# Rows of the moving operand padded to 2304 bytes per two chunks, and the high-weight products of a tile taken in the order xh, xh, xl, xl

## The chip, the cores and the metric

The kernel runs on one core of one Trainium2 chip. The metric is the device time of one execution in microseconds (us); lower is better. The times given are medians over several executions, and beside them stands one profiled execution with its own time.

## The reference

The kernel computes one inference step of a decoder with two layers for 256 prompt tokens and 8 sample tokens, which are handled together as 264 columns. Almost all of the work is products of float32 weights with activations of width 2048 (5632 in the hidden layer):

```python
h = rms_norm(x, norm_mix[layer])
z = h @ w_in                       # even layer 2048x4608, odd layer 2048x4112
y = mixer(z) @ w_out               # 2048x2048; attention+conv, or linear attention+pooling
x = x + y
h = rms_norm(x, norm_ffn[layer])
x = x + (silu(h @ w_gate) * (h @ w_up)) @ w_down     # 2048x5632, 2048x5632, 5632x2048
```

Each weight is used once for all 264 columns. It streams from HBM in float32.

## The kernel before

Activations stand with the features on the 128 partitions: a chunk is 128 features, and its row on each partition has T = 264 numbers of 4 bytes, 1056 bytes. An activation of width 2048 has 16 chunks, the hidden one has 44. To keep the accuracy of float32 each operand is split into a high part (rounded to the matmul's format `F32R`) and the rest: `xh` and `xl` for the normalised input, `hh` and `hl` for the input of the output projections and of the down projection, `whi` and `wlo` for the weights. Three products are summed: high weight by high activation, high weight by low activation, low weight by high activation.

The weights come in units. A unit is two chunks of the contraction by 512 output features (512 KB), loaded by SyncE's queue into one of four slots of `raw`; ScalarE writes its high part (`split_hi`, L404), VectorE the rest (`split_lo`, L413). TensorE then runs `unit`: for each of the four tiles `t` of 128 output features it issues four high-weight products (L514), over the two chunks `kk` and within each over the high and the low activation, and after the four tiles eight low-weight products (L520) follow, two per tile. So a unit has 16 + 8 = 24 matmuls of 128x128 weights by a 128x264 moving operand, each with its own weight load. Units that end a group with `single` set run the low products of a tile right behind its high ones. The sum of a tile stays in one PSUM bank over all units of its group: 8 units where the input has 16 chunks, 22 in the down projection. Index `j` below is the place of a unit in its group; it reads chunks 2j and 2j+1.

All buffers are placed by hand with `put`, one after another from byte 1024 of a partition:

```python
x = put("x", [P, KC, T], 1024)
xh_t = put("xh", [P, KC, T], after("x"), F32R)
xl_t = put("xl", [P, KC, T], after("xh"), F32R)
raw = put("raw", [P, RING, 2 * COLS], after("xl"))
```

This gives, with 1056 = 4 x 256 + 32 bytes a chunk, the byte offsets xh 17920 (70 x 256), xl 34816 (136 x 256), raw 51712, whi 68096 (266 x 256), wlo 84480, hh 100864 (394 x 256), hl 147328 (575 x 256 + 128). So chunk c of xh and of xl starts 32c bytes behind a multiple of 256, that of hh too, and that of hl 128 + 32c bytes behind one. Every weight tile starts at a multiple of 256.

The order of the work on each engine is the order of the code. TensorE waits at a unit for `hi_done` before the high products and for `lo_done` before the low ones.

Of the kernel before, what the change touches and what calls it, by code (L numbers as in the profile page):

```python
# [27 lines left out]
F32R = mybir.dt.float32r  # L28
# [6 lines left out]
P = 128  # L35
D = 2048
TP, NB = 256, 8
T = TP + NB
KC = D // P
# [9 lines left out]
PB = 15  # L49
COLS = 512  # L50
RING = 4
AHEAD = 3


# [80 lines left out]
def decoder_step(nc, a, o):  # L135
# [6 lines left out]
    with ctx:  # L142
        def sem(name):
            return ctx.enter_context(nc.semaphore(name))
# [5 lines left out]
        def put(name, shape, at, dt=F32):  # L150
            size = 1
            for s in shape[1:]:
                size *= s
            size *= 2 if dt == BF16 else 4
            used[name] = (at, at + size)
            return nc.alloc_sbuf_tensor_at(name, shape, dt, offset=at)

        def after(name):
            return (used[name][1] + 31) // 32 * 32

        x = put("x", [P, KC, T], 1024)
        xh_t = put("xh", [P, KC, T], after("x"), F32R)
        xl_t = put("xl", [P, KC, T], after("xh"), F32R)
        xh, xl = ([z[:, c, :] for c in range(KC)] for z in (xh_t, xl_t))
        raw = put("raw", [P, RING, 2 * COLS], after("xl"))
        whi = put("whi", [P, RING, 2 * COLS], after("raw"), F32R)
        wlo = put("wlo", [P, RING, 2 * COLS], after("whi"), F32R)
        hh = put("hh", [P, FC, T], after("wlo"), F32R)
# [79 lines left out]

        raw_full = [sem(f"raw_full{s}") for s in range(RING)]
        raw_up = [sem(f"raw_up{s}") for s in range(RING)]  # L250
        hi_done = sem("hi_done")
# [117 lines left out]
        def at_turn(eng, i, step, first):  # L369

            if i is None:
                return first
            return i * step + first if isinstance(i, int) else eng.snap(i * step + first)


        def pieces(buf, n, split=False):

            slot = buf[:, n % RING, :]  # L380
            if n >= U_EVEN + 2 * IN_UNITS:
# [8 lines left out]
        def split_hi(act, n, i=None, step=0, up=None):  # L390

            if beyond(n, i, step):
                return
            landed = at_turn(act, i, 16 * step // RING, 16 * (n // RING + 1))
            if up is not None:
                up = at_turn(act, i, up[1], up[0])
            free = at_turn(act, i, step, n - RING + 1)
            act.wait_ge(raw_full[n % RING], landed)
            if up is not None:
                act.wait_ge(raw_up[n % RING], up)  # L400
            if n >= RING:
                act.wait_ge(units_done, free)
            for dst, src in zip(pieces(whi, n, True), pieces(raw, n)):
                ins = act.activation(dst, src, ACT.Copy)  # L404
            ins.then_inc(hi_done, 1)
# [96 lines left out]
        def _(pe):  # L502
            def unit(n, yhi, ylo, k0, bank, first, last, i=None, step=0, taken=None, single=False):


                s = n % RING
                by_tile = single and last
                pe.wait_ge(lo_done if by_tile else hi_done, at_turn(pe, i, step, n + 1))

                def hi_part(t):  # L510
                    for kk in range(2):
                        c = kk * COLS + t * P
                        for m, r in enumerate((yhi, ylo)):
                            pe.matmul(ps[:, bank + t, 0:T], whi[:, s, c:c + P], r[k0 + kk],  # L514
                                      start=first and kk == 0 and m == 0, stop=False)

                def lo_part(t):
                    for kk in range(2):
                        c = kk * COLS + t * P
                        mm = pe.matmul(ps[:, bank + t, 0:T], wlo[:, s, c:c + P], yhi[k0 + kk],  # L520
                                       start=False, stop=last and kk == 1)
                    return mm

                for t in range(4):
                    if taken is not None and t < 3:
                        pe.wait_ge(evac_t, taken[0] + t)
                    if taken is not None and t == 3:
                        pe.wait_ge(evac_g, taken[1])
                    hi_part(t)
                    if by_tile:  # L530
                        mm = lo_part(t)
                        if t < 3:
                            mm.then_inc(tile_done, 1)
                if not by_tile:
                    pe.wait_ge(lo_done, at_turn(pe, i, step, n + 1))
                    for t in range(4):
                        mm = lo_part(t)
                mm.then_inc(units_done, 1)
# [393 lines left out]
        def _(act):  # L932
# [14 lines left out]
            def norm_prep(m, g, taken, base):  # L947

                c0 = 4 * g
                if m:  # L950
                    act.wait_ge(evac_g, taken)
                else:
                    act.wait_ge(d_x[g], 16)
                for t in range(2 if m == g == 0 else 0, 4):
                    ins = act.activation(xh[c0 + t], x[:, c0 + t, :], ACT.Copy, scale=vec[:, base + c0 + t:base + c0 + t + 1])  # L955
                ins.then_inc(xh_done, 1)
                if m or g > 1:
                    act.wait_ge(acc_done, 3 * m + max(g - 1, 0))
                act.activation(sqs[:, min(g, 1), :, :].rearrange("p c t -> p (c t)"),
                               x[:, c0:c0 + 4, :].rearrange("p c t -> p (c t)"), ACT.Square).then_inc(sq_done, 1)  # L960
# [59 lines left out]
            for u in range(EVEN_GROUPS * IN_UNITS):  # L1020
                n = U_EVEN + u + AHEAD
                split_hi(act, n)
# [73 lines left out]
            def out_proj(U, G, m, base, split_rows):  # L1096
                for q in range(4):
                    for j in range(IN_UNITS):
                        up = (16 * (q + 1), 0) if split_rows and (j + AHEAD) in ATTN_UNITS else None
                        split_hi(act, U + IN_UNITS * q + j + AHEAD, up=up)  # L1100
                    norm_prep(m, q, G + q + 1, base)

            def ffn(layer, U, G, m):
                def gate_up(i, peeled):
                    for k in range(2 * IN_UNITS):
                        split_hi(act, U + k + AHEAD, i=i, step=2 * IN_UNITS)
                        if peeled and k == 5:
# [12 lines left out]
                if layer == 0:  # L1120
                    for q in range(4):
                        for j in range(DN_UNITS):
                            split_hi(act, U2 + DN_UNITS * q + j + AHEAD)
                        norm_prep(2, q, G2 + q + 1, V_MIX + KC)
                    return

                for k in range(4 * DN_UNITS):
                    split_hi(act, U2 + k + AHEAD)
                    q, at = divmod(k, DN_UNITS)
# [729 lines left out]
```

## Time and profile before

| what | value |
|---|---|
| time, median of 3 | 2267.44 us (2267.36 to 2268.8) |
| time of the profiled execution | 2266.24 us |
| its span, first to last instruction | 2264.5 us |
| TensorE busy | 99% of the span |
| VectorE, ScalarE busy | 54%, 42% |
| granted TensorE clock, mean | 0.995 |
| matmuls | 18226 |

The span is the time in which the profile sees instructions; the time of the same execution is 1.74 us longer. A matmul is listed with its own duration (some 0.28 us), but matmuls overlap: what one costs in a stream is the distance from its start to the start of the next.

### The profile page before, as it was taken

What the parts mean: (1) busy time and instruction counts of PE and PEld (TensorE: products, weight loads), DVE (VectorE), ACT (ScalarE), POOL (GpSimd) and SP (SyncE); (2) the same over time, 40 slices, a digit from 0 to 9 for tenths busy, and PEclk for the clock granted to TensorE, in tenths of its full rate; (3) what the DMA queues carried; (4) which work ended last, traced back from release to release, by engine and by line L of the source; (5) the groups of instructions that cost most, each with busy time, mean ns of one, the idle gap of its engine ahead of it and who ended that gap; (6) DMA issues with size and microseconds to landing.
All of it is one profiled execution on the core that took longest, in us unless ns stands there. A gap on an engine that the chain in (4) does not pass through costs nothing.

```text
span 2264.5 us, 43613 instructions
## 1 busy us (share of the span) xinstructions
PE 2245.3 (99%) x18226; PEld 2222.4 (98%) x18226; DVE 1218.8 (54%) x1294; ACT 952.6 (42%) x1059; POOL 18.0 (1%) x20
## 2 busy tenths in 40 slices
PE   7999999999999999999999999999999999999999
PEld 7999999999999999999999999999999999999999
DVE  5777656555555554444465466565555555544443
ACT  6545345334343433433353335453434334343332
POOL 0000000000000000000000020000000000000000
PEclk9999999999999999999999999999999999999999
DMA  6654465655556565555564485556565655655654
GB/s 209 234 172 135 138 187 170 192 178 180 181 178 184 167 193 178 180 175 185 186 196 143 127 247 162 181 178 185 168 192 169 189 181 177 185 178 191 190 186 132
DMA packets 217579, 405.13 MB, mean 179 GB/s; under 512 B 15440, under 2 KB 29392, under 8 KB 217312
## 3 DMA queue, kind: packets, MB, share of 16 engines
q1 hardware_dynamic: 201360, 384.94, 55.0%
q10 hardware_dynamic: 16112, 18.63, 2.5%
q8 instruction: 83, 1.36, 0.2%
q14 instruction: 24, 0.20, 0.0%
HBM read 395.67 MB, written 9.93 MB: 179 GB/s over the span
## 4 chain that ended last, share of the span: by engine, by line
PE 97%; DVE 1%; ACT 1%; issue 0%; DMA 0%; SPq 0%; ACTq 0%; DVEq 0%
PE ps L514 62%; PE ps L520 31%; PE ps L848 1%; PE ps L819 0%; PE ps L816 0%; DMA raw<-in_w_in_even 0%; PE ps L858 0%; DVE wlo L413 0%; ACT whi L404 0%; PE ps L595 0%; PE ps L886 0%; PE ps L613 0%; PE ps L604 0%; PE ps L549 0%; ACT xh L955 0%
## 5 line engine op out<-in xcount | busy, mean ns | idle before, releaser
L413 DVE TENSOR_TENSOR wlo<-raw,whi 128x1024 fp32r<-128x1024 f32 (+1 forms) x746 | 886.0, 1202 | 837.2 <-ACT whi L404 836.2
L404 ACT ACTIVATE whi<-raw 128x1024 fp32r<-128x1024 f32 (+1 forms) x746 | 765.3, 1038 | 913.6 <-PE ps L520 902.2
L514 PE MATMUL ps<-xh,whi 128*128 128x264 f32 x3904 | 984.9, 288 | 10.1 <-ACT whi L404 9.1
L514 PE MATMUL ps<-xl,whi 128*128 128x264 f32 x3904 | 976.7, 285 | 0.0
L514 PEld LDWEIGHTS ps<-xh,whi 128*128 128x128 f32 x3904 | 740.6, 190 | 17.7 <-DVE xl L1335 8.5
L514 PEld LDWEIGHTS ps<-xl,whi 128*128 128x128 f32 x3904 | 741.6, 190 | 0.7
L520 PE MATMUL ps<-xh,wlo 128*128 128x264 f32 x3904 | 564.7, 285 | 0.0
L520 PEld LDWEIGHTS ps<-xh,wlo 128*128 128x128 f32 x3904 | 513.1, 189 | 0.0
L514 PE MATMUL ps<-hh,whi 128*128 128x264 f32 x1920 | 477.3, 284 | 1.1 <-DVE gbuf L1325 1.1
L514 PE MATMUL ps<-hl,whi 128*128 128x264 f32 x1920 | 477.2, 284 | 0.0
L514 PEld LDWEIGHTS ps<-hh,whi 128*128 128x128 f32 x1920 | 361.1, 188 | 1.3 <-issue 1.3
L514 PEld LDWEIGHTS ps<-hl,whi 128*128 128x128 f32 x1920 | 361.1, 188 | 0.0
L520 PE MATMUL ps<-hh,wlo 128*128 128x264 f32 x1920 | 273.0, 284 | 0.0
L520 PEld LDWEIGHTS ps<-hh,wlo 128*128 128x128 f32 x1920 | 250.1, 188 | 0.0
L1114 ACT ACTIVATE hh<-ubuf 128x1056 f32 (+1 forms) x22 | 23.9, 1087 | 101.3 <-DVE ubuf L1559 101.3
L1111 ACT ACTIVATE gbuf<-gbuf 128x1056 f32<-128x1056 f32 x22 | 23.9, 1087 | 66.5 <-DVE gbuf L1552 66.5
L1562 DVE TENSOR_TENSOR hl<-ubuf,hh 128x1056 f32 (+1 forms) x22 | 27.7, 1258 | 30.1 <-ACT hh L1114 30.1
L955 ACT ACTIVATE xh<-x,vec 128x264 fp32r<-128x264 f32 x62 | 26.9, 504 | 37.2 <-DVE x L1522 37.2
L1292 DVE SCALAR_TENSOR_TENSOR xl<-x,vec,xh 128x264 fp32r<-128x264 f32 x62 | 26.5, 489 | 22.6 <-ACT xh L955 22.6
L1554 DVE TENSOR_TENSOR ubuf<-ps,rstd 128x1056 f32<-128x1056 f32 x22 | 27.7, 1258 | 12.9 <-PE ps L520 12.9
L1552 DVE TENSOR_TENSOR gbuf<-ps,rstd 128x1056 f32<-128x1056 f32 x22 | 27.7, 1257 | 11.9 <-PE ps L520 11.9
L1559 DVE TENSOR_TENSOR ubuf<-ubuf,gbuf 128x1056 f32<-128x1056 f32 x22 | 27.7, 1258 | 2.5
(210 smaller groups left out, 582.2 us busy)
## 6 DMA issues: line engine op xcount, KB each, us to landing
raw<-in_w_gate SPq DMA_DIRECT2D x176, 512.0 KB, 4.0
raw<-in_w_up SPq DMA_DIRECT2D x176, 512.0 KB, 4.3
raw<-in_w_down SPq DMA_DIRECT2D x176, 512.0 KB, 3.7
raw<-in_w_in_even SPq DMA_DIRECT2D x72, 512.0 KB, 4.1
raw<-in_w_in_odd SPq DMA_DIRECT2D x66, 512.0 KB, 3.7
raw<-in_w_out_odd SPq DMA_DIRECT2D x32, 512.0 KB, 4.0
raw<-in_w_out_even SPq DMA_DIRECT2D x16, 512.0 KB, 4.5
raw<-in_w_out_even SPq DMA_DIRECT2D x32, 256.0 KB, 4.2
```

The lines of the kernel that those rows point to most:

```text
L404: ins = act.activation(dst, src, ACT.Copy)
L413: ins = dve.tensor_tensor(dst, src, hi.bitcast(F32), ALU.subtract)
L514: pe.matmul(ps[:, bank + t, 0:T], whi[:, s, c:c + P], r[k0 + kk], start=first and kk == 0 and m == 0, stop=False)
L520: mm = pe.matmul(ps[:, bank + t, 0:T], wlo[:, s, c:c + P], yhi[k0 + kk], start=False, stop=last and kk == 1)
L955: ins = act.activation(xh[c0 + t], x[:, c0 + t, :], ACT.Copy, scale=vec[:, base + c0 + t:base + c0 + t + 1])
L1111: act.activation(gbuf[:, :, :], gbuf[:, :, :], ACT.Silu).then_inc(silu_done, 1)
L1114: act.activation(dst, ubuf[:, :, :], ACT.Copy).then_inc(hh_done, 1)
L1292: ins = dve.scalar_tensor_tensor(xl[c], x[:, c, :], vec[:, base + c:base + c + 1], xh[c].bitcast(F32), ALU.mult, ALU.subtract)
L1552: dve.tensor_tensor(gbuf[:, :, :], ps[:, 0:4, 0:T], scale, ALU.mult).then_inc(evac_g, 1)
L1554: dve.tensor_tensor(ubuf[:, :, :], ps[:, 4:8, 0:T], scale, ALU.mult).then_inc(evac_g, 1)
L1559: dve.tensor_tensor(ubuf[:, :, :], ubuf[:, :, :], gbuf[:, :, :], ALU.mult).then_inc(h_ready, 1)
L1562: dve.tensor_tensor(hl[:, at, :], ubuf[:, :, :], hh[:, at, :].bitcast(F32), ALU.subtract).then_inc(hid_done, 1)
```

## The change

The rows of `xh` and `xl` are put in pairs of chunks, and each pair takes 576 numbers (2304 = 9 x 256 bytes) in place of 528 (2112 bytes). Each of the two buffers grows by 1536 bytes, and every buffer behind xh moves: xl starts at 36352 (142 x 256) and all behind it 3072 (12 x 256) bytes further. In `unit`, the two loops of the high products change places.

```diff
+PAIR = 576
...
-        xh_t = put("xh", [P, KC, T], after("x"), F32R)
-        xl_t = put("xl", [P, KC, T], after("xh"), F32R)
-        xh, xl = ([z[:, c, :] for c in range(KC)] for z in (xh_t, xl_t))
+        xh_t = put("xh", [P, KC // 2, PAIR], after("x"), F32R)
+        xl_t = put("xl", [P, KC // 2, PAIR], after("xh"), F32R)
+        xh, xl = ([z[:, c // 2, (c % 2) * T:(c % 2 + 1) * T] for c in range(KC)] for z in (xh_t, xl_t))
...
                 def hi_part(t):
-                    for kk in range(2):
-                        c = kk * COLS + t * P
-                        for m, r in enumerate((yhi, ylo)):
+                    for m, r in enumerate((yhi, ylo)):
+                        for kk in range(2):
+                            c = kk * COLS + t * P
                             pe.matmul(ps[:, bank + t, 0:T], whi[:, s, c:c + P], r[k0 + kk],
                                       start=first and kk == 0 and m == 0, stop=False)
```

After the change an even chunk of xh or xl starts at a multiple of 256 bytes and an odd one 32 bytes behind one, whatever the pair. The starts of hh and hl within 256 bytes stay what they were.

On TensorE, the end of the first unit of the even layer's input projection (the last tiles' high products, the low products, the start of the next unit) was this before; xh and xl are the two parts of the input, whi and wlo those of the weights:

```order
L514 MATMUL ps<-xl,whi 128x264
L514 MATMUL ps<-xh,whi 128x264
L514 MATMUL ps<-xl,whi 128x264
L514 MATMUL ps<-xh,whi 128x264
L514 MATMUL ps<-xl,whi 128x264
L520 MATMUL ps<-xh,wlo 128x264 x8
L514 MATMUL ps<-xh,whi 128x264
```

It is this after the change:

```order
L515 MATMUL ps<-xh,whi 128x264 x2
L515 MATMUL ps<-xl,whi 128x264 x2
L515 MATMUL ps<-xh,whi 128x264 x2
L515 MATMUL ps<-xl,whi 128x264 x2
L521 MATMUL ps<-xh,wlo 128x264 x8
L515 MATMUL ps<-xh,whi 128x264 x2
```

The two chunks of xh now come one after the other, then the two of xl; the same weight tile is no longer used by two matmuls in a row, and the eight low products keep their place.

The same place in the output projection of the even layer, on TensorE, where hh and hl are the two parts of the activation, was this before:

```order
L514 MATMUL ps<-hl,whi 128x264
L528 REGISTER_ALU
L514 MATMUL ps<-hh,whi 128x264
L514 MATMUL ps<-hl,whi 128x264
L514 MATMUL ps<-hh,whi 128x264
L514 MATMUL ps<-hl,whi 128x264
L520 MATMUL ps<-hh,wlo 128x264 x8
```

It is this after the change:

```order
L515 MATMUL ps<-hl,whi 128x264 x2
L529 REGISTER_ALU
L515 MATMUL ps<-hh,whi 128x264 x2
L515 MATMUL ps<-hl,whi 128x264 x2
L521 MATMUL ps<-hh,wlo 128x264 x8
```

Here only the order moved; the rows of hh and hl are not padded.

## Rows read from the trace of the kernel before

**Rows 1.** The page: busy time by engine, and TensorE's granted clock in 40 slices.

```profile
span 2264.5 us, 43613 instructions
PE 2245.3 (99%) x18226; PEld 2222.4 (98%) x18226; DVE 1218.8 (54%) x1294; ACT 952.6 (42%) x1059; POOL 18.0 (1%) x20
PEclk9999999999999999999999999999999999999999
```

**Rows 2.** The page's costliest groups: busy us, mean ns | idle before, releaser.

```profile
L413 DVE TENSOR_TENSOR wlo<-raw,whi 128x1024 fp32r<-128x1024 f32 (+1 forms) x746 | 886.0, 1202 | 837.2 <-ACT whi L404 836.2
L404 ACT ACTIVATE whi<-raw 128x1024 fp32r<-128x1024 f32 (+1 forms) x746 | 765.3, 1038 | 913.6 <-PE ps L520 902.2
...
L520 PE MATMUL ps<-xh,wlo 128*128 128x264 f32 x3904 | 564.7, 285 | 0.0
...
L520 PE MATMUL ps<-hh,wlo 128*128 128x264 f32 x1920 | 273.0, 284 | 0.0
```

**Rows 3.** Waits of TensorE: engine line, waited for, us in total, times, longest.

```profile
PE ps L514 <- ACT whi L404: 9.1, 2, 8.5
```

**Rows 4.** Timeline of TensorE, gate projection, units j = 0 to 5: start us, us.

```profile
435.78 0.28 PE L514 MATMUL ps<-xh,whi 128*128 128x264 f32 x1
...
437.70 1.13 PE L520 MATMUL ps<-xh,wlo 128*128 128x264 f32 x8
438.67 0.28 PE L514 MATMUL ps<-xh,whi 128*128 128x264 f32 x1
...
440.61 1.14 PE L520 MATMUL ps<-xh,wlo 128*128 128x264 f32 x8
441.58 0.29 PE L514 MATMUL ps<-xh,whi 128*128 128x264 f32 x1
...
443.54 1.15 PE L520 MATMUL ps<-xh,wlo 128*128 128x264 f32 x8
444.52 0.28 PE L514 MATMUL ps<-xh,whi 128*128 128x264 f32 x1
...
447.43 0.28 PE L514 MATMUL ps<-xh,whi 128*128 128x264 f32 x1
...
449.36 1.13 PE L520 MATMUL ps<-xh,wlo 128*128 128x264 f32 x8
450.32 0.28 PE L514 MATMUL ps<-xh,whi 128*128 128x264 f32 x1
```

**Rows 5.** Timeline of TensorE, down projection: units j = 20, 21, then 0 to 3.

```profile
937.04 0.28 PE L514 MATMUL ps<-hh,whi 128*128 128x264 f32 x1
...
939.94 0.28 PE L514 MATMUL ps<-hh,whi 128*128 128x264 f32 x1
...
942.85 0.28 PE L514 MATMUL ps<-hh,whi 128*128 128x264 f32 x1
...
944.79 1.12 PE L520 MATMUL ps<-hh,wlo 128*128 128x264 f32 x8
945.76 0.28 PE L514 MATMUL ps<-hh,whi 128*128 128x264 f32 x1
...
947.68 1.14 PE L520 MATMUL ps<-hh,wlo 128*128 128x264 f32 x8
948.66 0.29 PE L514 MATMUL ps<-hh,whi 128*128 128x264 f32 x1
...
950.61 1.14 PE L520 MATMUL ps<-hh,wlo 128*128 128x264 f32 x8
951.59 0.28 PE L514 MATMUL ps<-hh,whi 128*128 128x264 f32 x1
...
953.56 1.14 PE L520 MATMUL ps<-hh,wlo 128*128 128x264 f32 x8
954.54 0.28 PE L514 MATMUL ps<-hh,whi 128*128 128x264 f32 x1
```

## The prediction, made before the result was known

> **What bounds the kernel now.** I read the page first. TensorE is busy 99% of the span and its granted clock is at the upper level in all 40 slices; VectorE and ScalarE are busy 54% and 42% [rows 1]. The groups say whose turn it is: the high split of the weights on ScalarE was idle 902.2 us waiting for TensorE's low products, and VectorE 836.2 us waiting for that split [rows 2]. Both splitters run at TensorE's pace. TensorE itself waited for a split twice, 9.1 us in all, 8.5 of them in one wait [rows 3]. So the end is set by how fast matmuls follow one another, and nothing else that this change touches can give or take much unless TensorE begins to wait.
>
> How fast do they follow? The timeline shows it, by the distances of starts. In the gate projection six units start at 435.78, 438.67, 441.58, 444.52, 447.43 and 450.32 [rows 4]: 2.89, 2.91, 2.94, 2.91 and again 2.89 us for 24 matmuls each, although each does the same work on the same shapes. In the down projection units j = 0 to 3 take 2.91, 2.90, 2.93 and 2.95 us [rows 5]. The one thing that runs in a cycle of four units is the place of the rows within 256 bytes: chunk c starts 32c bytes behind a multiple of 256, so units of j = 0 and 4 read rows at 0 and 32, j = 1 at 64 and 96, j = 2 at 128 and 160, j = 3 at 192 and 224.
>
> Is it the rows' place, or a beat of four that TensorE keeps by itself? The down projection tells: its group has 22 units, no multiple of four. Units 20 and 21 take 2.90 and 2.91 us, and then the next group's j = 0 and 1 take 2.91 and 2.90 us; a beat of its own would have gone on with the 2.93 and 2.95 us that come two units later [rows 5]. The pattern starts anew with the rows. I read it so: what one matmul costs depends, by some per cent of 121 ns, on where its moving row and its neighbours' begin within 256 bytes.
>
> **The change part by part.**
>
> *Padding.* After it every unit on xh and xl reads rows at 0 and 32, as only the units j = 0 and 4 do today. A cycle of four units takes 447.43 - 435.78 = 11.65 us, 2.9125 a unit; the two units with rows at 0 and 32 take 2.89 and 2.89 [rows 4]. The number of units on xh is 3904 low products by 8 = 488 [rows 2]. At 2.89 us for all the gain is 0.0225 x 488 = 11.0 us. The starts are given to 0.01 us, so this term is good to about 0.005 x 488 = 2.4 us.
>
> *Order, on xh and xl.* The high products now read rows at 0, 32, 0, 32 with a new weight tile each time. That is exactly the pattern of the eight low products today. With rows at 0 and 32 those take 438.67 - 437.70 = 0.97 and 450.32 - 449.36 = 0.96 us [rows 4], 0.965 on average; three times that is a unit of 2.895 us. Today's order gives 2.89. I take 2.893: a gain of 0.0195 x 488 = 9.5 us. Giving up the repeated weight tile costs nothing visible: high products that repeat theirs and low ones that do not run alike, (437.70 - 435.78) / 16 = 0.120 us against 0.965 / 8 = 0.121.
>
> *Order, on hh and hl.* These rows do not move within 256 bytes, but the order is new: with hl 128 bytes off, a tile reads rows at 0, 128, 32, 160 today and at 0, 32, 128, 160 afterwards (j = 0; the others shifted). No row of this trace shows that order. The nearest rows: today's high products take 1.94, 1.92, 1.95 and 1.97 us for j = 0 to 3, mean 1.945; the low ones, another order of the same rows, take 0.97, 0.98, 0.98, 0.98, mean 0.978, which is 1.955 for sixteen [rows 5]; and the high ones on xh, a third order, take 1.92, 1.94, 1.96 in the units j = 0 to 2 [rows 4]. Three orders average to within 1% of each other, so I take no change. The bounds are the best and the worst single unit, 1.92 and 1.97 us, for all of the 1920 / 8 = 240 units [rows 2]: 6 us less or 6 us more.
>
> *The shift of all buffers behind xh* is 3072 bytes, a multiple of 256; by the reading above it costs nothing. The pairs j = 0 and j = 4 lie 8448 bytes apart, a multiple of 256 but of no higher power of two, and take the same 2.89 us [rows 4]; so the address bits above 256 have shown no effect. If they had, it would come as in the no-change rival.
>
> *What else.* No wait is added and no instruction either: the writers of xh and xl write rows of the same length, the transfers are the same, and which sum closes when is unchanged. With a unit 0.02 us shorter, the splitters have less idle time: a whi split takes 1.038 us and a wlo split 1.202 us a unit [rows 2], far below 2.89; their idle time covers it 80 times over.
>
> The sum: 9.5 us off the profiled execution's 2266.24 gives 2256.7; the median of the runs lies 1.2 us above that execution, so I expect 2257.9 us, 0.4% faster.
>
> **A rule that speaks against it.** The trace shows matmuls of 264 columns 2.89 / 24 = 0.120 to 2.94 / 24 = 0.1225 us apart by the rows they read [rows 4]. The Trainium skill, "TensorE: Matmul & The Clock Gate", section "Back-to-back issue gap", makes the distance a matter of the column count alone. Its formula, as an estimate from that page, gives 112.5 ns for 264 columns; the trace does not agree, with 120 ns at the least. By that rule the padding would do nothing and the time would stay at 2267.4 us; the first rival is that outcome.
>
> **The rivals.**
>
> *No change.* The cause of the cycle is not the row's place within 256 bytes but something that goes with it, such as the distance between row and weight tile or the two buffers' distance, which the new layout does not reproduce; then units average 2.9125 us as now and the time is 2267.4 us. For it: I have only a pattern, no mechanism. Against it: units 20 and 21 against 0 and 1, and j = 0 against j = 4. The Trainium skill, "SBUF — State Buffer", section "Specifications (TRN2)", speaks of lines of 16 bytes only; by them rows that all start at multiples of 32 are alike. The trace does not agree, by 2.89 against 2.94 us.
>
> *Slower.* The mechanism is the order: where two matmuls in a row no longer share a weight tile, and the row alternates between places, each high product falls to the slowest pace seen, 1.97 us for sixteen [rows 5]. A unit on xh would take 1.97 + 0.965 = 2.935 us, 0.0225 more than now, times 488 = 11.0 us; a unit on hh 1.97 in place of 1.945, times 240 = 6 us; together 2284 us. It decides from 2.9125 - 0.965 = 1.9475 us for the sixteen high products of an xh unit, against the 1.93 I expect. For it: on hh the order is unseen. Against it: the low products have this very form and are not slow at 0 and 32.
>
> *Larger gain.* The new order also avoids the slow neighbours on hh, and each of its units takes the 1.92 us of the best: 6 us more, and with 2.89 on xh 1.5 more, gives 2250.4 us. For it: hl stands 128 bytes off hh, and today's order jumps between them at each matmul. Against it: the low products never jump and are no faster.
>
> **How the numbers follow.** A measurement of this kernel tells about 0.2%, 4.5 us, from no change. The forecast, 2257.9, has a chance of 0.60; its own range is 2253 to 2263, from 2.4 us of rounding and half of the 6 us of the order on hh. The larger gain has 0.18, no change 0.13, slower 0.09. The range 2249 to 2266 takes in the forecast, the larger gain, and losses on hh that eat most of the gain; it leaves out 2267 and above. Faster 0.77: nearly all of the first two cases, less a little where hh takes its 6 us; same 0.14; slower 0.09.
>
> **What would show it.** After the change the starts of units on xh should be 2.89 to 2.90 us apart for every j, without the cycle of four. If the cycle is still there, the place within 256 bytes is not the cause. If the cycle is gone but at 2.91 or more, the order costs. On hh the low products should still take 0.97 to 0.98 us, and the high ones an average of 1.945; a new average there is the order's own effect. The clock should stay at the upper level and TensorE's wait for the splits near 9 us; more of it would mean that I was wrong about what covers them. The prediction fails most simply if hh loses what xh gains.

## The result, and the profile after

The changed kernel takes 2256.45 us (median of 5, 2254.95 to 2259.57) against 2267.39 us (median of 5); the ratio is 0.9955, interval 0.9944 to 0.9966. It is 0.45% or 10.9 us faster; 2257.9 us was forecast, 0.4%. The range held the time and the sign was right. One reason behind it was not, as the experiments show.

The profiled execution took 2259.57 us, one of the longer ones. Its page, where the lines of [rows 1] stand, reads:

```profile
span 2257.8 us, 43613 instructions
PE 2237.8 (99%) x18226; PEld 2214.4 (98%) x18226; DVE 1217.8 (54%) x1294; ACT 952.4 (42%) x1059; POOL 18.1 (1%) x20
PEclk9999999999999999999999899999999999999999
```

TensorE is still the bound, with the same 18226 matmuls. A 9 in the clock's row stands for 90% or more of a slice, so neither this row nor that of [rows 1] shows whether the clock fell for a few microseconds. TensorE's waits for the high split are as small as in [rows 3], 9.4 us in two waits.

From here on one reading serves for all kernels: the start of a unit of the gate projection, and the start of the one 64 units later; and the start of the down projection's first unit, and that of the one 44 units (two whole groups) later. Their distances divided by 64 and by 44 are the mean unit on xh and on hh, good to a fraction of a nanosecond. The timeline of TensorE in the kernel before (start us, us) has, beside the start at 435.78 of [rows 4]:

```profile
622.23 0.28 PE L514 MATMUL ps<-xh,whi 128*128 128x264 f32 x1
...
878.61 0.28 PE L514 MATMUL ps<-hh,whi 128*128 128x264 f32 x1
...
1007.09 0.28 PE L514 MATMUL ps<-hh,whi 128*128 128x264 f32 x1
```

That is 186.45 / 64 = 2.9133 us a unit on xh and 128.48 / 44 = 2.9200 on hh. The same view of the changed kernel:

```profile
434.76 0.28 PE L515 MATMUL ps<-xh,whi 128*128 128x264 f32 x1
...
619.08 0.28 PE L515 MATMUL ps<-xh,whi 128*128 128x264 f32 x1
...
872.52 0.28 PE L515 MATMUL ps<-hh,whi 128*128 128x264 f32 x1
...
1001.60 0.29 PE L515 MATMUL ps<-hh,whi 128*128 128x264 f32 x1
```

A unit on xh takes 184.32 / 64 = 2.8800 us, 120.0 ns a matmul; one on hh 129.08 / 44 = 2.9336, more than before. With all units of a kind taken like the ones measured, the 488 units on xh give 0.0333 x 488 = 16.3 us and the 240 on hh take back 0.0136 x 240 = 3.3 us: 13.0 us net.

The two profiled executions differ by 6.7 us only. The windows say where the rest is. Their columns are: stretch, length, TensorE busy (matmuls), granted clock, DMA share, GB/s. Before the change:

```profile
240.00:280.00 40.00, 40.00 (x312) 0.91 0.44 121
1225.00:1300.00 75.00, 75.00 (x525) 0.93 0.39 120
```

After it:

```profile
240.00:280.00 40.00, 40.00 (x298) 0.87 0.45 123
1225.00:1300.00 75.00, 75.00 (x502) 0.86 0.39 119
```

These are the two places where the stream of projections is mixed with the mixers' small products, and the clock falls there to its lower level (1.2 GHz) for some microseconds, in both kernels; from 245.10 to 248.30 us the kernel before had a granted clock of 0.50. If TensorE does half as much in that time, a stretch loses its length times the missing share: 40 x 0.09 + 75 x 0.07 = 8.9 us before and 40 x 0.13 + 75 x 0.14 = 15.7 after, 6.8 us more in this execution. Taken from the 13.0 us this leaves 6.2, and 6.7 was measured. The mean clocks of the five runs of the changed kernel were 0.992 to 0.994, its shortest run having the highest; a few microseconds of this kind differ from run to run.

### The profile page after: what moved, and what is told of

Same layout as the page of the kernel before. It is cut to its first block, busy times and chain, and to the rows that moved or that the text cites. A ratio compares the mean times of both kernels' runs of the same rounds, so it can differ in the third digit from the quotient of the medians.

```text
span 2257.8 us, 43613 instructions
## 1 busy us (share of the span) xinstructions
PE 2237.8 (99%) x18226; PEld 2214.4 (98%) x18226; DVE 1217.8 (54%) x1294; ACT 952.4 (42%) x1059; POOL 18.1 (1%) x20
## 4 chain that ended last, share of the span: by engine, by line
PE 96%; DVE 1%; ACT 1%; DMA 1%; issue 0%; SPq 0%; ACTq 0%; DVEq 0%
PE ps L515 61%; PE ps L521 30%; DMA raw<-in_w_in_even 1%; PE ps L849 1%; PE ps L820 0%; PE ps L817 0%; ACT whi L405 0%; DVE wlo L414 0%; PE ps L859 0%; PE ps L596 0%; PE ps L887 0%; PE ps L614 0%; PE ps L605 0%; PE ps L550 0%; ACT xh L956 0%
## 5 line engine op out<-in xcount | busy, mean ns | idle before, releaser
L515 PE MATMUL ps<-xh,whi 128*128 128x264 f32 x3904 | 802.2, 287 | 10.7 <-ACT whi L405 9.4
L515 PE MATMUL ps<-xl,whi 128*128 128x264 f32 x3904 | 794.1, 285 | 0.0
L515 PEld LDWEIGHTS ps<-xh,whi 128*128 128x128 f32 x3904 | 606.7, 190 | 19.1 <-DVE xl L1336 8.3
L515 PEld LDWEIGHTS ps<-xl,whi 128*128 128x128 f32 x3904 | 605.5, 190 | 0.0
L521 PE MATMUL ps<-xh,wlo 128*128 128x264 f32 x3904 | 559.0, 284 | 0.0
L521 PEld LDWEIGHTS ps<-xh,wlo 128*128 128x128 f32 x3904 | 507.3, 189 | 0.0
L515 PE MATMUL ps<-hh,whi 128*128 128x264 f32 x1920 | 391.3, 285 | 1.3 <-DVE gbuf L1326 1.3
L515 PE MATMUL ps<-hl,whi 128*128 128x264 f32 x1920 | 391.4, 285 | 0.0
L515 PEld LDWEIGHTS ps<-hh,whi 128*128 128x128 f32 x1920 | 298.3, 189 | 1.5 <-issue 1.5
L515 PEld LDWEIGHTS ps<-hl,whi 128*128 128x128 f32 x1920 | 298.6, 189 | 0.0
```

## The experiments

A time with an interval is a median of several; where one time stands alone, the unit times, which do not depend on the clock's falls elsewhere, are the better measure. A "place" is the start of a row in bytes behind a multiple of 256.

### Padding alone, order alone

`pad_only` is the changed kernel with the old loops:

```diff
-                    for m, r in enumerate((yhi, ylo)):
-                        for kk in range(2):
-                            c = kk * COLS + t * P
+                    for kk in range(2):
+                        c = kk * COLS + t * P
+                        for m, r in enumerate((yhi, ylo)):
```

> The padded rows with the old order xh, xl, xh, xl. Theory 1 (the rows' place within 256 bytes alone sets the pace): every unit on xh at 2.88 to 2.89 us, units on hh unchanged at 2.91, 2.90, 2.93, 2.95; time 2255 to 2257 us, at or below the changed kernel since hh loses nothing. Theory 2 (place and order act together): units on xh at 2.89 us as today's j = 0, of which the order takes another 0.012 us in the changed kernel; time about 2257.

Measured: 2266.1 us, ratio 0.9998, interval 0.9989 to 1.0007. The padding alone gives nothing. Timeline of TensorE:

```profile
434.99 0.28 PE L515 MATMUL ps<-xh,whi 128*128 128x264 f32 x1
...
436.94 1.12 PE L521 MATMUL ps<-xh,wlo 128*128 128x264 f32 x8
437.90 0.28 PE L515 MATMUL ps<-xh,whi 128*128 128x264 f32 x1
...
621.44 0.28 PE L515 MATMUL ps<-xh,whi 128*128 128x264 f32 x1
```

186.45 / 64 = 2.9133 us a unit, to the digit the mean of before. But the cycle of four is gone: the unit shown takes 437.90 - 434.99 = 2.91, and so do the others. The low products are at their best (0.96 us for eight), the sixteen high ones take 1.95 where the same rows in the same order took 1.92 before the change [rows 4, j = 0]. So both theories were wrong here. The rows' places count, since the cycle went with them, but the two rows of a unit do not settle what it takes. Either what was read before it counts too (unit j = 0 of the unpadded kernel comes behind the places 192 and 224), or the distance between the buffers does; `old_apart_512` and `hl_place_timed` below decide.

`order_only` is the kernel before with the new loops.

> The new order with unpadded rows. Theory 1 (place alone): the cycle of four stays on xh with a mean of 2.91 us, and hh goes to the 2.93 us of the changed kernel; time 2269 to 2271 us. Theory 2 (the order by itself quickens units, place hardly counts): units on xh near 2.88 us without a cycle, time about 2257 us.

Measured: 2270.0 us, ratio 1.0015, interval 1.0006 to 1.0024: slower by 0.15%, in the range of theory 1.

```profile
436.65 0.28 PE L514 MATMUL ps<-xh,whi 128*128 128x264 f32 x1
...
623.31 0.28 PE L514 MATMUL ps<-xh,whi 128*128 128x264 f32 x1
...
879.98 0.28 PE L514 MATMUL ps<-hh,whi 128*128 128x264 f32 x1
...
888.79 0.41 PE L514 MATMUL ps<-hh,whi 128*128 128x264 f32 x2
...
891.72 0.41 PE L514 MATMUL ps<-hh,whi 128*128 128x264 f32 x2
...
1009.12 0.29 PE L514 MATMUL ps<-hh,whi 128*128 128x264 f32 x1
...
1017.89 0.40 PE L514 MATMUL ps<-hh,whi 128*128 128x264 f32 x2
...
1020.79 0.41 PE L514 MATMUL ps<-hh,whi 128*128 128x264 f32 x2
```

Units on xh take 186.66 / 64 = 2.9166 us, those on hh 129.14 / 44 = 2.935. Neither edit gives anything alone; together they give 16 us on xh. The loss on hh belongs to the order.

Two things here go beyond theory 1. On xh the cycle has eight units, not four: j = 2 starts at 442.48 and j = 3 at 445.42 (2.94 us), but j = 6 at 454.12 and j = 7 at 457.08 (2.96 us), with rows at the same places; it comes back in every group. And on hh the same unit has two times. The first and the third group of the down projection read the same rows from the same slots into the same banks, yet the first four units take 891.72 - 879.98 = 11.74 us in the one and 1020.79 - 1009.12 = 11.67 us in the other, and the fourth of them still 2.93 against 2.90. Apart from the values of the weights, only what ran before differs: the up projection, or another group on hh. So its effect reaches over at least three whole units, 72 matmuls.

### New order on xh, old order on hh

`order_x_only` is the changed kernel with the choice made by the operand:

```diff
-                    for m, r in enumerate((yhi, ylo)):
-                        for kk in range(2):
+                    for kk, m in (((0, 0), (1, 0), (0, 1), (1, 1)) if yhi is xh else ((0, 0), (0, 1), (1, 0), (1, 1))):
+                            r = (yhi, ylo)[m]
```

> Padded rows; new order for units on xh, old order for units on hh. If the two kinds of units are independent: xh units 2.880 us as in the changed kernel, hh units 2.92 us on average as before, so 0.01 us x 240 = 2.5 us below the changed kernel: about 2254 us. If the loss on hh came from the moved buffers and not from the order, hh units stay at 2.93 us and the time is that of the changed kernel, 2256.

Measured: 2252.09 us, ratio 0.9930, interval 0.9917 to 0.9944.

```profile
434.54 0.28 PE L515 MATMUL ps<-xh,whi 128*128 128x264 f32 x1
...
618.86 0.28 PE L515 MATMUL ps<-xh,whi 128*128 128x264 f32 x1
...
872.30 0.28 PE L515 MATMUL ps<-hh,whi 128*128 128x264 f32 x1
...
1000.79 0.28 PE L515 MATMUL ps<-hh,whi 128*128 128x264 f32 x1
```

184.32 / 64 = 2.8800 us on xh and 128.49 / 44 = 2.9202 on hh: the gain on xh without the loss on hh. The moved buffers have no part in the loss on hh.

### Place against what?

`place_128` moves the rows of xh and xl by 128 bytes and leaves the weights where they are within 256 bytes; `all_128` moves everything behind x by 128:

```diff
-        xh_t = put("xh", [P, KC // 2, PAIR], after("x"), F32R)
+        xh_t = put("xh", [P, KC // 2, PAIR], after("x") + 128, F32R)
...
-        raw = put("raw", [P, RING, 2 * COLS], after("xl"))
+        raw = put("raw", [P, RING, 2 * COLS], after("xl") + 128)     # place_128 only
```

> The changed kernel with xh and xl begun 128 bytes further, so that all pairs have rows at 128 and 160; weights and hh stay at their places within 256. If the place relative to the weights or to the 256 bytes counts: units on xh rise from 2.880 towards the 2.94 us of today's j = 2, all alike, and the time to about 2275 us or less. If only the equality of all pairs counts, they stay at 2.880 us and the time at 2256.

> The changed kernel with every buffer behind x 128 bytes further, weights and hh too. If the place counts relative to the weight tiles: units on xh at 2.880 us and the four units on hh unchanged (2.946, 2.927, 2.937, 2.937 us for j = 0 to 3), time 2257 us. If the place counts by itself: xh units at 2.960 us as in the kernel with the rows alone moved, the values of hh rotated by two, time about 2284 us.

Measured, one time each: 2283.76 us with the rows alone moved, 2253.92 us with everything moved. TensorE's timeline with the rows alone moved:

```profile
438.21 0.29 PE L515 MATMUL ps<-xh,whi 128*128 128x264 f32 x1
...
627.65 0.29 PE L515 MATMUL ps<-xh,whi 128*128 128x264 f32 x1
```

With everything moved:

```profile
431.98 0.28 PE L515 MATMUL ps<-xh,whi 128*128 128x264 f32 x1
...
616.30 0.28 PE L515 MATMUL ps<-xh,whi 128*128 128x264 f32 x1
...
869.74 0.28 PE L515 MATMUL ps<-hh,whi 128*128 128x264 f32 x1
...
998.81 0.29 PE L515 MATMUL ps<-hh,whi 128*128 128x264 f32 x1
```

189.44 / 64 = 2.960 us against 184.32 / 64 = 2.8800, and hh at 129.07 / 44 = 2.9334, the value of the changed kernel. So it is not the row's own address that counts but its place against the weight tiles, which moved along in the second kernel and not in the first. The slow case is slower than expected: 2.960 us is more than the 2.94 of any unit in [rows 4], and 2283.76 us more than the 2275. Equal pairs alone are no merit, since at places 128 and 160 all units are equally slow.

### The distance of the buffers

`apart_512` is the changed kernel with `put("xl", ..., after("xh") + 512)`, `old_apart_512` is `pad_only` with the same. They were to say why sixteen high products took 1.92 us at j = 0 before and 1.95 with the padding alone.

> The changed kernel with xl and all behind it 512 bytes further, so that xl starts 18944 bytes behind xh (512 more than a multiple of 2048, as before the change) and not 18432 (a multiple of 2048). Theory 3 (the distance of two rows read in turn counts by its bits above 256): units on xh rise from 2.880 to the 2.906 us that the order-only kernel had at j = 0, in every unit, 0.026 x 488 = 12.7 us in all, about 2269 us. Theory 1 (place within 256 bytes alone, given the order): 2.880 us and about 2257 us.

> Padded rows, old order, xl 512 bytes further. Theory 3: each unit on xh takes the 2.892 us of j = 0 before the change, in place of 2.913 with the padding alone; 0.021 x 488 = 10 us, about 2256 us. If the distance has no part in it: 2.913 us and 2266 us.

Measured, one time each: 2255.86 and 2269.34 us. Timeline of `apart_512`:

```profile
432.47 0.28 PE L515 MATMUL ps<-xh,whi 128*128 128x264 f32 x1
...
616.79 0.28 PE L515 MATMUL ps<-xh,whi 128*128 128x264 f32 x1
```

And of `old_apart_512`:

```profile
436.16 0.28 PE L515 MATMUL ps<-xh,whi 128*128 128x264 f32 x1
...
622.62 0.28 PE L515 MATMUL ps<-xh,whi 128*128 128x264 f32 x1
```

184.32 / 64 = 2.8800 and 186.46 / 64 = 2.9134 us, both unchanged. Theory 3 fell: 512 bytes more between the buffers do nothing. Other distances were not tried.

### hl at the same place as hh

`hl_place` is `order_x_only` with one more edit:

```diff
-        hl = put("hl", [P, FC, T], after("hh"), F32R)
+        hl = put("hl", [P, FC, T], after("hh") + 128, F32R)
```

> New order on xh and old order on hh, with hl begun 128 bytes further, so that a chunk of hl stands at the same place within 256 bytes as that of hh. If hh then behaves as xh did before the change (same places, old order): 2.913 us a unit on average in place of 2.920, 0.007 x 240 = 1.7 us less than the kernel it is built from, about 2250.5 us. If the new distance between hh and hl is a worse one: 2.93 us or more, about 2255 us.

> The kernel with new order on xh, old order on hh and hl moved by 128 bytes, timed in rounds. By its units (2.880 us on xh, 2.9135 on average on hh and hl) against those before (2.9135 and 2.9215): 0.0335 x 488 + 0.008 x 240 = 18.3 us less, 2249 us.

Measured: 2248.01 us (one time), and for the same kernel as `hl_place_timed` 2248.39 us, ratio 0.9915, interval 0.9902 to 0.9929. The timeline of the latter:

```profile
432.03 0.28 PE L515 MATMUL ps<-xh,whi 128*128 128x264 f32 x1
...
616.35 0.28 PE L515 MATMUL ps<-xh,whi 128*128 128x264 f32 x1
...
869.79 0.28 PE L515 MATMUL ps<-hh,whi 128*128 128x264 f32 x1
...
881.46 0.28 PE L515 MATMUL ps<-hh,whi 128*128 128x264 f32 x1
...
884.35 0.28 PE L515 MATMUL ps<-hh,whi 128*128 128x264 f32 x1
...
933.88 0.29 PE L515 MATMUL ps<-hh,whi 128*128 128x264 f32 x1
...
936.79 0.28 PE L515 MATMUL ps<-hh,whi 128*128 128x264 f32 x1
...
997.97 0.29 PE L515 MATMUL ps<-hh,whi 128*128 128x264 f32 x1
```

128.18 / 44 = 2.913 us on hh. With the same places and the same order hh takes what xh took before the change, 2.9133. 128 unused bytes are worth 0.007 x 240 = 1.7 us.

The same lines show what `pad_only` left in doubt. Unit j = 4 starts at 881.46, behind one with rows at 192 and 224, and takes 2.89 us. Unit j = 0 of the second group starts at 933.88, behind j = 21 with rows at 64 and 96, and takes 2.91. Both read rows at 0 and 32 in the same order, in one kernel: a unit's time depends on what was read before it.

`hl_place_new_order` has the new order everywhere on top of this layout.

> The new order on all units, padded xh and xl, hl moved by 128 bytes. Theory 4 (the sequence of places within 256 bytes, relative to the weight tile, sets the pace, whatever the buffer): units on hh take what the order-only kernel took on unpadded xh, 2.906, 2.928, 2.960, 2.886 us for j = 0 to 3, mean 2.920; time 2250 us. If the buffer or its distance mattered: other values, such as the 2.937 us of the changed kernel, and 2254 us.

Measured: 2249.05 us (one time).

```profile
869.77 0.28 PE L515 MATMUL ps<-hh,whi 128*128 128x264 f32 x1
...
998.12 0.28 PE L515 MATMUL ps<-hh,whi 128*128 128x264 f32 x1
```

128.35 / 44 = 2.917 us, which is the 2.9166 of unpadded xh in the new order. Theory 4 holds: the same sequence of places gives the same time, whichever buffer it is. The values expected for single j did not come one by one, since the cycle has eight units here too, as in `order_only`.

### Cheaper padding

`x_blocks` is `hl_place` with xh and xl in blocks of four chunks, 1088 numbers each, begun 192 bytes further, so that units alternate between places 192, 224 and 0, 32. It asks whether a third of the padding would do.

```diff
-        xh_t = put("xh", [P, KC // 2, PAIR], after("x"), F32R)
+        xh_t = put("xh", [P, KC // 4, 4 * T + 32], after("x") + 192, F32R)
...
+        xh, xl = ([z[:, c // 4, (c % 4) * T:(c % 4 + 1) * T] for c in range(KC)] for z in (xh_t, xl_t))
+        raw = put("raw", [P, RING, 2 * COLS], after("xl") + 64)
```

> xh and xl in blocks of four chunks, 4352 = 17 x 256 bytes each, begun 192 bytes behind a multiple of 256: even units read rows at 192 and 224, odd units at 0 and 32, for 1024 bytes of padding a buffer pair of 2048 less than the changed kernel's. Theory 4a (each of these two pairs of places runs at 120 ns and a switch between them costs nothing lasting): 2.880 to 2.886 us a unit, about 2248 us. Theory 4b (a switch costs, as in the order-only kernel, where j = 0 took 2.906 us after j = 3): up to 2.906 us a unit, 0.02 x 488 = 10 us more, about 2258 us.

Measured: 2258.14 us (one time).

```profile
432.21 0.28 PE L515 MATMUL ps<-xh,whi 128*128 128x264 f32 x1
...
435.11 0.41 PE L515 MATMUL ps<-xh,whi 128*128 128x264 f32 x2
...
438.02 0.41 PE L515 MATMUL ps<-xh,whi 128*128 128x264 f32 x2
...
618.02 0.28 PE L515 MATMUL ps<-xh,whi 128*128 128x264 f32 x1
```

185.81 / 64 = 2.9033 us: theory 4b. Changing the pair of places from unit to unit costs 0.023 us a unit, two thirds of the gain. It is not that only the pair 192 and 224 is slow: the unit from 435.11 to 438.02 reads rows at 0 and 32 and takes 2.91 us, where it takes 2.88 when all units read there. No run has 192 and 224 alone.

### Sequence of places or repeated weight tile?

The new order differs from the old in two things: the places alternate, and no weight tile is used twice in a row. `side_by_side` parts them. It is `hl_place` with the old order everywhere and this layout:

```diff
-        xh_t = put("xh", [P, KC // 2, PAIR], after("x"), F32R)
-        xl_t = put("xl", [P, KC // 2, PAIR], after("xh"), F32R)
-        xh, xl = ([z[:, c // 2, (c % 2) * T:(c % 2 + 1) * T] for c in range(KC)] for z in (xh_t, xl_t))
+        xhl = put("xl", [P, KC, PAIR], after("x"), F32R)
+        xh, xl = ([xhl[:, c, m * T:(m + 1) * T] for c in range(KC)] for m in range(2))
```

> The chunk of xh and that of xl lie side by side in 2304 bytes, so that every chunk of xh is at place 0 and every one of xl at place 32; old order everywhere, hl moved by 128 bytes. High products on xh then read places 0, 32, 0, 32 as in the changed kernel, but each weight tile is used twice in a row as before the change; low products read 0, 0. Theory 5 (the sequence of places alone): sixteen high products in 1.920 us, as in the changed kernel. Theory 6 (using a weight tile twice in a row is what cost 1.952 us with the padding alone): 1.95 us again. With low products at 0.960 us the units take 2.880 or 2.913 us and the time is 2248 or 2264 us.

Measured: 2248.3 us, ratio 0.9912, interval 0.9896 to 0.9929. xh and xl are one buffer here, which the trace calls xl:

```profile
432.32 0.28 PE L514 MATMUL ps<-xl,whi 128*128 128x264 f32 x1
...
435.20 2.08 PE L514 MATMUL ps<-xl,whi 128*128 128x264 f32 x16
437.12 1.12 PE L520 MATMUL ps<-xl,wlo 128*128 128x264 f32 x8
438.08 2.08 PE L514 MATMUL ps<-xl,whi 128*128 128x264 f32 x16
...
616.64 0.28 PE L514 MATMUL ps<-xl,whi 128*128 128x264 f32 x1
```

Sixteen high products take 437.12 - 435.20 = 1.92 us, eight low ones 0.96, a unit 184.32 / 64 = 2.8800. Each weight tile is used twice in a row, as before the change, and the pace is that of the changed kernel. Theory 5 holds, theory 6 falls, for rows at 0 and 32; other places were not tried this way. The low products read place 0 only, and run at 120 ns too. So the old order gives the whole gain if the two chunks' places are laid out for it; for this kernel the order of the loops and the layout are one choice.

## Why the prediction was right, and where it was not

**What bounds the kernel, and that nothing else changes**: right. The same instructions, waits of TensorE near 9 us, and the time goes where the starts of matmuls say.

**Padding, 11.0 us at 2.89 us a unit**: the step that failed. It took unit j = 0's 2.89 us for a property of its two rows and carried it to all units. With the padding alone and the old order, the units all have rows at j = 0's places and take 2.913. The sequence 0, 0, 32, 32 costs 1.92 or 1.95 us for sixteen matmuls depending on what ran before. That the forecast stood was luck in this part: the other edit, forecast as a small loss, supplied together with the padding what the padding was credited with.

**Order on xh, a loss of 1.5 us against the padding**: wrong in sign. Given the padded rows, the order is what brings the unit from 2.9133 to 2.8800. The observation under it, that high products would then read as the low ones do, was right: those ran at 0.965 for eight at places 0 and 32, and in an unbroken sequence of them at 0.960. The two terms together were forecast at 9.5 us and measured 16.3.

**Order on hh, no change**: mis-sized; 3.3 us slower, inside the 6 us given as bound. Three orders that average to the same did not make the fourth do so. This and the extra 6.8 us on xh offset each other in part, and of the 13.0 us that the units give the median shows 10.9. The lower clock is the likely rest, not shown run by run: the mean clock had a median of 0.993 in the five runs of the changed kernel and 0.994 in 21 runs of the kernel before, and a thousandth is 2.3 us.

**The shift by 3072 bytes costs nothing**: right; `order_x_only` has hh at its old 2.920 us, and 128 bytes for all buffers change nothing either (2.8800 and 2.9334 us).

**The rivals.** No change: it did not come, but the cause that it named is part of the truth. It spoke of the distance between row and weight tile, and `place_128` and `all_128` show that this distance within 256 bytes is what counts; the new layout kept it, since every weight tile stands at a multiple of 256. The rule of the Trainium skill, "TensorE: Matmul & The Clock Gate", section "Back-to-back issue gap", has a formula by the columns alone, as an estimate 112.5 ns for 264; the section gives it for a matmul in isolation, which the prediction left out. The runs do not agree: 120.0 to 123.3 ns (2.8800 to 2.960 us by 24) with nothing changed but addresses. Slower: its mechanism was half there; the order without the padding is slower, by 0.15%. It was named for a repeated weight tile, and `side_by_side` showed that with rows at 0 and 32 this has no part in it. Larger gain: on xh it came, on hh the opposite.

What stays open: why the places 0 and 32 against the weight tile run smoothly and 128 and 160 do not, how long the effect of earlier matmuls lasts beyond the three units seen, and whether it makes the cycle of eight or an address bit above 256 does. Padding hh and hl the same way in `hl_place` would bring 0.033 x 240 = 8 us more, an estimate from 2.913 and 2.880 us; it needs 2 x 22 x 192 = 8448 bytes a partition. It wasn't tried. Whether the larger share of lower clock in the changed kernel is due to it or to the run was not settled: other kernels' profiled runs had 0.992 (`old_apart_512`, old order) to 0.995 (`place_128` and `all_128`, new order).

## What to carry to other kernels

When TensorE is the bound and units of equal work differ by a few nanoseconds a matmul in a fixed cycle, look at where the moving rows start against the weight tiles, counted within 256 bytes, and measure units by the distance of two starts many units apart. Such a cost belongs to the sequence, not to the operand: test layout and order together and apart, and choose the order for each operand. A fast unit in a slow cycle is no promise of what all would do in its place.

## What was not expected of the hardware

Matmuls of 264 columns in the F32R format ran 120.0 ns apart at best, and up to 123.3 ns with rows 128 bytes further against their weight tiles. In streams whose units all read the same two places, the place within 256 bytes was enough to tell the cost: the units of the changed kernel lie 9 x 256 bytes apart and all take 2.880 us, 512 bytes between the buffers changed nothing, 128 bytes for all buffers together changed nothing, while 128 bytes for the rows alone cost 0.08 us a unit. Where the places change from unit to unit it was not enough: in `order_only` the units j = 2 and j = 6 took 2.94 and 2.96 us with rows at the same places. Mean unit times repeated to a nanosecond over kernels: 2.9133 us on xh before the change, with the padding alone, and again on hh (2.913) once hl stood at hh's place.
